# Splitting the tokens of a product-key expert layer: 80 by gathered rows on VectorE, 176 by dense plain float32 products

## What is computed

```python
def chunk(hc):                     # 128 tokens
    q = (hc @ wq).reshape(T, PEER_HEADS, 2, PEER_KEY_DIM)
    s1 = jnp.einsum('thd,hnd->thn', q[:, :, 0], sub_keys[:, 0])
    s2 = jnp.einsum('thd,hnd->thn', q[:, :, 1], sub_keys[:, 1])
    v1, i1 = lax.top_k(s1, PEER_TOPK)
    v2, i2 = lax.top_k(s2, PEER_TOPK)
    cand = (v1[..., :, None] + v2[..., None, :]).reshape(T, PEER_HEADS, PEER_TOPK * PEER_TOPK)
    sc, ci = lax.top_k(cand, PEER_TOPK)
    e = i1[ci // PEER_TOPK] * PEER_NKEYS + i2[ci % PEER_TOPK]     # take_along_axis
    g = jax.nn.softmax(sc, axis=-1)
    act = jax.nn.gelu(jnp.einsum('td,thkd->thk', hc, exp_u[e]), approximate=False)
    return jnp.einsum('thk,thkd->td', g * act, exp_v[e])
```

## Time and profile before

| | |
|---|---|
| median of three runs | 965.26 us |
| span of the profiled execution | 962.4 us |
| PE busy | 941.5 us |
| DVE busy | 715.6 us |
| ACT busy | 475.2 us |
| GpSimd busy | 123.7 us |
| moved by DMA | 192.61 MB, mean 200 GB/s |
| instructions | 16211 |

### The profile page before, as it was taken

One profiled execution on the slowest core, in us unless ns is written; L12 is line 12 of the kernel. 1 busy time (PEld: TensorE's weight loads), 2 busy tenths in 40 slices (PEclk: granted clock), 3 DMA queues, 4 the chain that ended last, 5 costly groups with the idle time before them and its releaser, 6 DMA issues.

```text
span 962.4 us, 16211 instructions
## 1 busy us (share of the span) xinstructions
PE 941.5 (98%) x6378; PEld 855.2 (89%) x6378; DVE 715.6 (74%) x1260; ACT 475.2 (49%) x827; POOL 123.7 (13%) x70
## 2 busy tenths in 40 slices
PE   6999999999999999999999999999999999999997
PEld 4988798899999999999999999888888888888785
DVE  5959797559999978888899985555555555686656
ACT  4553665354444545454444444544455544455454
POOL 2000000069889800000000000000000000000000
PEclk9999999999999999999999999999999999999999
DMA  9998745126565554454545455566656666965553
GB/s 345 367 412 347 321 184 226 59 72 191 179 182 190 177 176 153 154 159 154 168 157 155 154 159 190 179 195 197 194 191 188 195 195 195 369 197 187 182 191 121
DMA packets 48797, 192.61 MB, mean 200 GB/s; under 512 B 5297, under 2 KB 7505, under 8 KB 47442
## 3 DMA queue, kind: packets, MB, share of 16 engines
q1 hardware_dynamic: 48626, 191.52, 59.0%
q0 software_dynamic: 96, 0.05, 0.0%
HBM read 190.48 MB, written 1.07 MB: 199 GB/s over the span
## 4 chain that ended last, share of the span: by engine, by line
PE 89%; DVE 4%; SPq 3%; DMA 2%; ACT 1%; issue 1%; POOL 0%; ACTq 0%; DVEq 0%
PE banks L1149 23%; PE banks L1124 13%; PE banks L1128 13%; PE banks L1125 12%; PE banks L1156 12%; PE banks L1140 3%; PE banks L784 2%; DMA win<-in_w_in 2%; PE banks L851 1%; PE banks L804 1%; PE banks L789 1%; SPq L366 1%; DVE sc_w L1268 1%; PE banks L760 1%; PE banks L1104 1%
## 5 line engine op out<-in xcount | busy, mean ns | idle before, releaser
L1561 DVE TENSOR_TENSOR lo<-raw,hi 128x1024 fp32r<-128x1024 f32 x213 | 266.4, 1252 | 165.0 <-ACT hi L660 164.9
L660 ACT ACTIVATE hi<-raw 128x1024 fp32r<-128x1024 f32 x255 | 270.2, 1060 | 170.1 <-PE banks L1156 170.1
L1124 PE MATMUL banks<-h2r,hi 128*128 128x256 f32 x1024 | 253.7, 285 | 0.0
L1125 PE MATMUL banks<-h2r,hi 128*128 128x256 f32 x1024 | 251.0, 283 | 0.0
L1149 PE MATMUL banks<-hi,wsplit 128*128 128x512 f32 x992 | 245.6, 390 | 0.5 <-DVE wsplit L1653 0.5
L1149 PEld LDWEIGHTS banks<-hi,wsplit 128*128 128x128 f32 x992 | 186.1, 188 | 39.8 <-issue 1.2
L1125 PEld LDWEIGHTS banks<-h2r,hi 128*128 128x128 f32 x1024 | 196.4, 192 | 0.0
L1124 PEld LDWEIGHTS banks<-h2r,hi 128*128 128x128 f32 x1024 | 196.1, 191 | 0.0
L466 POOL TENSOR_TENSOR lo<-raw,hi 128x1024 fp32r<-128x1024 f32 x42 | 118.6, 2838 | 208.9 <-ACT hi L660 208.6
L1128 PE MATMUL banks<-h2r,lo 128*128 128x256 f32 x1024 | 143.8, 283 | 0.2 <-POOL lo L466 0.2
L1156 PE MATMUL banks<-lo,wsplit 128*128 128x512 f32 x496 | 132.6, 389 | 0.0
(11 more groups left out here) (243 smaller groups left out, 937.5 us busy)
## 6 DMA issues: line engine op xcount, KB each, us to landing
raw<-in_u_t SPq DMA_DIRECT2D x128, 512.0 KB, 3.6
raw<-in_v_b SPq DMA_DIRECT2D x128, 512.0 KB, 3.5
wq<-in_wq SPq DMA_DIRECT2D x2, 4096.0 KB, 18.2
sh_w<-in_w_mod SPq DMA_DIRECT2D x8, 512.0 KB, 13.2
sc_w<-in_w_mod SPq DMA_DIRECT2D x8, 512.0 KB, 13.3
win<-in_w_in SPq DMA_DIRECT2D x8, 512.0 KB, 14.2
win<-in_w_in SPq DMA_DIRECT2D x1, 4096.0 KB, 21.3
sc_w<-in_w_mod SPq DMA_DIRECT2D x2, 2048.0 KB, 23.6
```

What stands on the lines that cost most here:

```text
L660: nc.scalar.activation(high_at(n), raw[n % RAW][:, :], ACT.Copy).then_inc(high_ready, 1)
L1124: nc.tensor.matmul(dst, w, h2r[:, 0, c, :], start=(c == 0), stop=False)
L1125: nc.tensor.matmul(dst, w, h2r[:, 1, c, :], start=False, stop=False)
L1561: nc.vector.tensor_tensor(lo_t[n % RAW][:, :], raw[n % RAW][:, :], high_at(n).bitcast(F32), ALU.subtract).then_inc(vector_low, 1)
```

## The change

The 256 tokens are split. The last 80 of them (`FEW`, tokens 176 to 255, all in token tile 1) leave the dense products; the first 176 (`MANY`) stay in them.

- **Dense part.** No tile is split any more: PE multiplies the raw tiles with h2 (`hT`), in plain float32. `u_block` is 8 products of 176 columns. `v_block` has the raw tile as the stationary operand and `act[:, j, :]` of 176 columns as the moving one, 8 products; the sums stand transposed, features on the partitions (`chunk_place`). `high`, `low`, `whigh`, `wlow` and GpSimd's subtractions are gone. The gates are for 176 tokens: 22 groups, one every third block (`EVERY`) from block 56 on.
- **Gathered part.** The tile-1 tokens are sorted first. DVE computes the expert numbers, GpSimd writes them to DRAM and reads them back spread over the partitions: 64 tokens are paired (two partitions a token, 64 tiles), 16 are spread (8 partitions a token, 16 tiles). GpSimd then issues 160 indirect DMAs, each of 128 rows of 4 KB: 80 tiles of `u_rows` (a second copy of `exp_u` in the input, rows in plain order), then 80 of `v_b`. For a u tile DVE makes one fused product and sum with the token's h2 (`dot`); for a v tile it adds the tile times its weights to a sum (`weigh_rows`). Tiles go through 4 slots for the first 12, and 10 afterwards. 12 dots are put into the second sort, 4 ahead of the gates, one or two in each step of the u stretch, the rest and all weighings after it.
- **h2 of the 80** is turned to rows by 8 transposes at block 4, copied by ACT, and sent through DRAM to the two layouts.
- **Gate 2** is loaded at v blocks 63 to 70, summed when the weighings reach tile 60, and spread at v block 100.
- **The end.** The sums of the 80 tokens are folded by two products with 0/1 matrices (`few_sums`); after each finished chunk of the dense sums ACT copies it and PE turns it to rows (`to_rows`) into the same banks; residual and squares go in three pieces of columns (`PIECES`). PE waits before it for all 160 tiles (`rows_used`) and for gate 2.
- Constants moved with it: `EXP_AT` 38 to 46, `TURN_AT` 47 to 52, `GATE_AT` 53 to 56. Some semaphores are merged and several tiles lie elsewhere.

The core of the diff:

```diff
-HI = 3
-WS = 3
+PAIRED = 64
+SPREAD = 16
+FEW = PAIRED + SPREAD
+MANY = SEQ - FEW
+FEW0 = P - FEW
+TILES = PAIRED + SPREAD
+GATHERS = 2 * TILES
+EARLY_SLOTS = 4
+EARLY = 12
+SLOTS = 10
...
-EXP_AT = 38
-POOL_LOW = 46
-SORT_LOW = (15, 19, 24, 42)
-TURN_AT = 47
-GATE_AT = 53
+H2_AT = 4
+EXP_AT = 46
+SORT_SKIP = 2
+TURN_AT = 52
+GATE_AT = 56
+EVERY = 3
 GT = 8
 PT = 2
 GQ = GT // PT
-NG = SEQ // GT
+NG = MANY // GT
 GP = 2
 GATE_SCALE = 2.0 ** 14
-G2_LOAD = 82
-G2_SUM = 84
-G2_ROW = 104
+G2_LOAD = 63
+G2_SUM = 60
+G2_ROW = 100
+G2_GATE = 76
+BEFORE_GATES = 4
...
+        def slot_of(i):
+
+            return i % EARLY_SLOTS if i < EARLY else (i - EARLY + EARLY_SLOTS) % SLOTS
...
-            for n in range(POOL_LOW):
-                if n in SORT_LOW:
-                    continue
-                pool.wait_ge(high_ready, n + 1)
-                nc.gpsimd.tensor_tensor(lo_t[n % RAW][:, :], raw[n % RAW][:, :], hi_t[:, n % HI, :].bitcast(F32),
-                                        ALU.subtract).then_inc(pool_low, 1)
+            pool.wait_ge(xn_ready, TT + 3)
+            pool.dma_start(h2_lines.ap(), h2_stage[0:FEW, :]).then_inc(lines_moved, 16)
+            pool.wait_ge(lines_moved, H2_SAVED)
+            for k in range(P // PAIRED):
+                pool.dma_start(h2_pair[k * PAIRED:(k + 1) * PAIRED, :],
+                               bass.AP(tensor=h2_lines, offset=0, ap=[[D, PAIRED], [1, D]])).then_inc(lines_moved, 16)
+            pool.dma_start(h2_spread[:, :],
+                           bass.AP(tensor=h2_lines, offset=PAIRED * D, ap=[[0, P // SPREAD], [D, SPREAD], [1, D]])
+                           ).then_inc(lines_moved, 16)
+
+            def spread_lines(dst, lines):
+
+                for k in range(P // PAIRED):
+                    pool.dma_start(dst[k * PAIRED:(k + 1) * PAIRED, 0:PAIRED],
+                                   bass.AP(tensor=lines, offset=k * PAIRED, ap=[[HK, PAIRED], [1, PAIRED]])
+                                   ).then_inc(lines_moved, 16)
+                pool.dma_start(dst[:, PAIRED:TILES],
+                               bass.AP(tensor=lines, offset=PAIRED * HK,
+                                       ap=[[SPREAD, P // SPREAD], [HK, SPREAD], [1, SPREAD]])).then_inc(lines_moved, 16)
+
+            pool.wait_ge(chosen_ready, 1)
+            pool.dma_start(expert_lines.ap(), e_u[FEW0:P, :]).then_inc(lines_moved, 16)
+            pool.wait_ge(lines_moved, EXPERTS_SAVED)
+            spread_lines(idx, expert_lines)
+            pool.wait_ge(lines_moved, IDX_IN)
+            for i in range(GATHERS):
+                if i == EARLY:
+                    pool.wait_ge(chosen_ready, 2)
+                    pool.dma_start(gate_lines.ap(), chosen[FEW0:P, 1, 2, :]).then_inc(lines_moved, 16)
+                if i == EARLY + 4:
+                    pool.wait_ge(lines_moved, FEW_SAVED)
+                    spread_lines(gate_few, gate_lines)
+                if last_user(i) is not None:
+                    pool.wait_ge(rows_used, last_user(i) + 1)
+                k = i % TILES
+                nc.gpsimd.indirect_dma_start(out=rows[slot_of(i)][:, :], out_offset=None,
+                                             in_=u_rows if i < TILES else v_rows,
+                                             in_offset=bass.IndirectOffsetOnAxis(ap=idx[:, k:k + 1], axis=0)
+                                             ).then_inc(gathered[slot_of(i)], 16)
...
-                pe.wait_ge(high_ready, n + 1)
+                pe.wait_ge(raw_full[n % RAW], 16 * (n // RAW + 1))
                 if n >= 2:
                     pe.wait_ge(act_out, n - 1)
-                dst = bank[4 + n % 2][:, 0:SEQ]
+                dst = bank[4 + n % 2][:, 0:MANY]
                 for c in range(DC):
-                    w = hi_t[:, n % HI, c * P:(c + 1) * P]
-                    nc.tensor.matmul(dst, w, h2r[:, 0, c, :], start=(c == 0), stop=False)
-                    nc.tensor.matmul(dst, w, h2r[:, 1, c, :], start=False, stop=False)
-                low_ready(n)
-                for c in range(DC):
-                    last = nc.tensor.matmul(dst, lo_t[n % RAW][:, c * P:(c + 1) * P], h2r[:, 0, c, :],
-                                            start=False, stop=(c == DC - 1))
+                    last = nc.tensor.matmul(dst, raw[n % RAW][:, c * P:(c + 1) * P], hT[:, c, 0:MANY],
+                                            start=(c == 0), stop=(c == DC - 1))
                 last.then_inc(block_used, 1)
...
+            def v_part(j, c):
+
+                return nc.tensor.matmul(chunk_place(c), raw[(BLOCKS + j) % RAW][:, c * P:(c + 1) * P], act[:, j, :],
+                                        start=(j == 0 and c < 4), stop=(j == BLOCKS - 1), skip_group_check=True)
...
+            def few_sums(k):
+
+                cols = PIECES[k]
+                out = rows_at(1, k)[:, 0:cols.stop - cols.start]
+                nc.tensor.matmul(out, fold_pair[:, :], sum_pair[:, cols], start=True, stop=False, skip_group_check=True)
+                nc.tensor.matmul(out, fold_spread[:, :], sum_spread[:, cols], start=False, stop=False,
+                                 skip_group_check=True)
+
+            def to_rows(c):
+
+                pe.wait_ge(chunk_out, c + 1)
+                k = [n for n, cols in enumerate(PIECES) if cols.start <= c * P < cols.stop][0]
+                here = slice(c * P - PIECES[k].start, (c + 1) * P - PIECES[k].start)
+                nc.tensor.transpose(rows_at(0, k)[:, here], turned[:, c, 0:P], ident[:, :])
+                nc.tensor.matmul(rows_at(1, k)[0:FEW0, here], turned[:, c, P:MANY], ident[:, :], start=False,
+                                 stop=(here.stop == PIECES[k].stop - PIECES[k].start), skip_group_check=True
+                                 ).then_inc(columns_ready, 1)
...
+                if n == H2_AT:
+                    for c in range(DC):
+                        last = nc.tensor.transpose(bank[c // 4][0:FEW, c % 4 * P:(c % 4 + 1) * P], hT[:, c, MANY:SEQ],
+                                                   ident[:, :])
+                    last.then_inc(x2T_ready, 1)
...
+            pe.wait_ge(weight_ready, 2)
+            pe.wait_ge(rows_used, GATHERS)
+            pe.wait_ge(rows_read, 3)
+            few_sums(0)
+            few_sums(1)
+            for c in range(DC):
+                if c >= 4:
+                    pe.wait_ge(chunk_out, c - 3)
                 for j in range(BLOCKS - LAST, BLOCKS):
-                    last = v_part(j, 1, half)
+                    if c == 0:
+                        v_ready(j)
+                    last = v_part(j, c)
                 last.then_inc(peer_ready, 1)
+                if c == DC - 2:
+                    pe.wait_ge(chunk_out, DC - 2)
+                    few_sums(2)
+                if c:
+                    to_rows(c - 1)
+            to_rows(DC - 1)
...
+            def dot(i):
+
+                if i in (0, PAIRED):
+                    ve.wait_ge(lines_moved, H2_IN)
+                tile = row_tile(i)
+                nc.vector.tensor_tensor_reduce(out=tile, in0=tile, in1=h2_pair[:, :] if i < PAIRED else h2_spread[:, :],
+                                               scale=1.0, scalar=0.0, op0=ALU.mult, op1=ALU.add,
+                                               accum_out=dots[:, i:i + 1]).then_inc(rows_used, 1)
...
+            def weigh_rows(i):
+
+                k = i - TILES
+                total = sum_pair if k < PAIRED else sum_spread
+                tile = row_tile(i)
+                if k in (0, PAIRED):
+                    ve.wait_ge(weight_ready, 3 if k == 0 else 4)
+                    ins = nc.vector.tensor_scalar(total[:, :], tile, weight[:, k:k + 1], None, ALU.mult)
+                else:
+                    ve.wait_ge(rows_used, i)
+                    ins = nc.vector.scalar_tensor_tensor(out=total[:, :], in0=tile, scalar=weight[:, k:k + 1],
+                                                         in1=total[:, :], op0=ALU.mult, op1=ALU.add)
+                ins.then_inc(rows_used, 1)
...
+            def dot_in_sort():
+
+                places[0] += 1
+                if places[0] > SORT_SKIP and dotted[0] < EARLY:
+                    some_dots(1)
+
+            for n, t in enumerate((1, 0)):
+                between = dot_in_sort if n else (lambda: None)
...
+            onehots(0)
+            some_dots(BEFORE_GATES)
+            for n in range(GATE_AT + 1, BLOCKS + 2):
                 if GATE_AT < n - 1 < BLOCKS:
                     late(n - 1)
-                if group_at(n - 1 - GATE_AT) is not None:
-                    gate_acts(group_at(n - 1 - GATE_AT))
-                if n + 2 < STREAM:
-                    low(n + 2)
-                if n + 2 == BLOCKS + 1:
-                    ve.wait_ge(late_act, BLOCKS - 2 - GATE_AT)
-                    wlow(0)
-                if n == BLOCKS:
-                    ve.wait_ge(late_act, BLOCKS - 1 - GATE_AT)
-                if n + 2 > BLOCKS and n + 2 < STREAM:
```

(49 more changed lines are left out.)

378 lines of the change are left out of this document (169 added, 209 removed).

## The result

The kernel after takes 895.47 us in the median of four runs (894.68 to 899.00), the kernel before 964.97 beside it: a ratio of 0.9287 with an interval of 0.9261 to 0.9312. That is 70 us faster, inside the range of 852 to 900, but 25 us above the forecast of 870; the nearest case of the prediction is rival 1 (891).

What follows compares the result with a forecast made beforehand. TensorE was taken as the bound: 856.8 us span if only PE counts, plus 3 (turn) and 8 (DMA) gives 867.8, plus 2.9 around the span gives 870.7, rounded to 870 us; range 852 to 900.

Steps and rivals of the forecast that it cites:

- rival 1: V stretch: streams starve while gathers run, 405 GB/s shared evenly; about 29 us lost in place of 8, 891 us; chance 0.20.
- The plain product, 150 ns a record: Dense products on TensorE: 150 ns a record at 176 columns, 16 records, 2.40 us a block.
- rival 2: Dense products: plain product pays the split ones' 13 ns, 2.56 us a block; 41 us more, 911 us; chance 0.05.
- TensorE's sum to the start of v: U blocks, gates and transposes add 330.2 us to the first stream's start at 203.1: v blocks start at 533.3 us.
- The wait at block 52, 3 us: PE's turn at block 52 waits for VectorE's second sort, delayed by dots waiting for gathers: 3 us, bounds 0 and 10.
- The cost of a gather: GpSimd's issue of one indirect gather: 2.4 us taken, between bounds of 1.2 and 4.56 us.
- 2 to 3 us apart: Sign the prediction named for its forecast: gathers 2 to 3 us apart in the v stretch.
- Rival 4: Late gathers set the end beyond 3.5 us each; 880 to 958 us (chance 0.07), or slower, from 974 us (0.06).
- DMA, 8 us: V stretch: PE waits for raw tiles while gate 2 loads beside gathers; 8 us, bounds 0 and 35.
- the 9.6 us of lead: Gate 2 stretch: four buffers of lead, 9.6 us, cover part of SP's late loads.
- the dots would leave the gathers alone: Read from the skill: VectorE's two-port forms block GpSimd's descriptor writes, but tensor_tensor is not named, so dots do not disturb gathers.
- The end: After the v blocks: few_sums 3.4 us, last four blocks 9.6, turning back 2.7, then 8.5 after PE ends.

Runs made afterwards that it cites:

- experiment 1: The kernel after without the 80 gathers of v rows (80 tokens' output then not the reference's), one execution: 862.17 us.

## Why the prediction was right or wrong

- **The plain product, 150 ns a record**: right. 150.2 in u, 149.2 in v; rival 2 is out, although 2.56 us a block did appear. The prediction named 2.56 with no idle time as the sign of rival 2, and that sign was bad: the even split gives the same number, by 0.524 MB / 204.5 GB/s. The window with both counts tells them apart, and experiment 1.
- **TensorE's sum to the start of v**: 533.3 forecast, 534.1 came. Gate groups 0.92 instead of 0.97 us; one wait for a raw tile of 1.4 us at 225 to 237 us was not in it.
- **The wait at block 52, 3 us**: 0. The timeline of VectorE after:

```profile
325.79 0.42 DVE L1726 TENSOR_TENSOR chosen<-gate,gsum 128x256 f32<-128x256 f32 x1
...
330.53 0.56 DVE L1768 COPY chosenT<-banks 128x384 f32<-128x384 f32 x1 [3.71 <-PE banks L1246]
```

VectorE had `chosen` ready at 326.2 and waited itself for PE, which came to the turn at 330.09. The gathers came earlier than charged: the write of the experts and the reads back took 8 us instead of up to 11, and the first dot started at 270.6. The prediction's working for VectorE is also off by itself: 203.8 + 53.4 is 257.2, not 257.7, and the second sort is called the same as the first and taken as 54.6. Neither mattered, since PE came last.
- **The cost of a gather**: 2.4 us was taken. Its issue takes GpSimd 0.94 us at best, 1.20 us in the mean for the rows of u and 1.04 for those of v, at or under the lower bound of 1.2 (which was a time of its bytes and not of GpSimd). GpSimd and VectorE in the v stretch, first before gate 2's loads, then in them:

```profile
596.59 1.29 DVE L1650 SCALAR_TENSOR_TENSOR sum_pair<-rows,weight,sum_pair 128x1024 f32<-128x1024 f32 x1 [1.27 <-DMA rows<-in_v_b,idx]
598.15 0.94 POOL L532 DMA_INDIRECT rows<-in_v_b,idx  x1 [1.62 <-DVE sum_pair L1650]
599.15 1.28 DVE L1650 SCALAR_TENSOR_TENSOR sum_pair<-rows,weight,sum_pair 128x1024 f32<-128x1024 f32 x1 [1.27 <-DMA rows<-in_v_b,idx]
600.71 0.94 POOL L532 DMA_INDIRECT rows<-in_v_b,idx  x1 [1.62 <-DVE sum_pair L1650]
...
716.91 1.28 DVE L1297 SCALAR_TENSOR_TENSOR acc_g<-g_w,cact,acc_g 128x1024 f32<-128x1024 f32 x1
717.27 1.74 POOL L532 DMA_INDIRECT rows<-in_v_b,idx  x1 [0.83 <-DVE sum_pair L1650]
718.26 1.28 DVE L1650 SCALAR_TENSOR_TENSOR sum_pair<-rows,weight,sum_pair 128x1024 f32<-128x1024 f32 x1
```

The gathers of 598 and 600 us are 2.56 us apart, so "2 to 3 us apart" came true by the share of the DMA engines and not by GpSimd. Rival 4 fell with it: the weighings were over by about 753 us, 114 us before few_sums.
- **DMA, 8 us**: the step that failed in size. The mechanism was the one forecast, to the place of gate 2; it measured 33.3. Three numbers in it were wrong. The ceiling is 409 GB/s, not 430: the 446 of a 7 us window was let pull up what lasts, where the row of 10 us at 405 stood beside it. The even split was charged to gate 2 only; at 409 a block already takes 2.56 us with nothing of gate 2 about, and these 11 us (14 with those inside gate 2's stretch) were put at 0. And the 9.6 us of lead were subtracted from the gate 2 stretch, when the even split had used them up before it: PE waited at 569 to 580 us, more than 100 us earlier. Rival 1 had the first two right and subtracted the lead as well; its 29 us and 891 are the nearest of all cases.
- **The two rows where the Trainium skill was weighed.** The prediction read out of the Trainium skill, "SBUF — State Buffer", Who interferes with whom, that the dots would leave the gathers alone. The trace does not bear that out. The issues of 0.94 us above lie between two weighings (the one before ends at 597.88 us, the next starts at 599.15); the one of 1.74 us lies beside VectorE's. Of all 160 issues, the 98 with no dot, weighing or gate sum of VectorE (L1628, L1650, L1297) beside them took 0.94 to 1.09 us, and of the 62 others the longest took 1.99. So work of VectorE on two operands of SBUF does go with a longer issue, as rival 4 had feared, but by 1.05 us at most, which leaves it under the 2.56 us between gathers; the transfers stood at 409 GB/s all the while, so it cost nothing here. The other row: 44 blocks and 44 gathers went through in the same 112.7 us. The trace so agrees with the Trainium skill, "DMA: Bandwidth & Descriptors", Queues, rings and completion order, which has each DMA engine take turns between the rings with work. The prediction noted that this rule points to rival 1 at 405 GB/s and left that case at a chance of 0.20; with both queues always full, which the slots and VectorE's 1.28 us allowed, it deserved the most.
- **The end**: from few_sums to the last instruction 26.5 us, 24.2 forecast. The last four blocks run at 1.85 us a chunk with its turning back, where the sum had 1.2 + 0.33. Around the span 1.8 us, 2.9 forecast. Sum of all: 870.7 + 0.8 - 3 + 25.3 + 2.3 - 1.1 = 895.0, the profiled run's 894.99. One term carries the whole miss. That the time still lies in the range of 852 to 900 is owed to the range taking in rival 1, and not to the sum.

## What to carry to other kernels

When a change adds bytes beside a stream that PE lives on, add up the demand per block and hold it against the longest flat row of the rate, not against its peak; above it, both queues got half here, and a lead of a few buffers is gone long before the stretch you worry about. Then the cure is in the order and not in the engines: moving 4 MB to where the gathers are over gave 18 us, and spreading the gathers to 386 GB/s another 8, 869.3 us in all, 26 less than the kernel after. An operation that waits for another engine must not stand in front of work that this engine will wait for: gate 2, harmless with 80 gathers, made VectorE stand for 64 us and TensorE for 82 when there were 160.

## What the runs showed of the hardware

- Loads from HBM into SBUF by two or three queues stood at 409 to 411 GB/s wherever both kinds of queue were full (409 from 534 to 757 us in the kernel after), whatever the mix of plain and indirect transfers; one stream alone took the 220 that it asked for.
- Indirect gathers of 128 rows of 4 KB beside plain loads of the same size moved as many bytes: 44 and 44 tiles in 112.7 us. With no stream beside them they followed each other every 1.39 us, the pace of VectorE's weighings; how fast they go without those was not measured.
- The issue of a gather takes GpSimd 0.94 us, and up to 1.99 us beside operations of VectorE on two operands of SBUF (98 and 62 of the 160 issues).
- The share goes by queue: 1 to 1 with one hardware queue, 44 to 38 with two, where the stream was satisfied.
- A plain float32 product is two records of 150 ns at 176 columns, and the three blocks at 705.80, 716.04 and 726.28 us, each after 2.47 us of waiting, had a mean granted clock of 0.60 and took 4.31 us in place of 2.65. The block at 700.68 us, after 2.57 us, still ran at 2.4 GHz.
